# A two-block transformer step on one core: split weights in a ring of 512-row chunks, projections by token halves, attentions begun among the value blocks

## The reference, cut to what matters

```python
def hybrid_layer(x, w_in, w_out, ...):          # layers 0 and 1
    proj = x @ w_in                              # 1024 x 3352
    y = concat(retention(...), nsa(...), rg_lru(...))
    return layer_norm(ALPHA * x + y @ w_out, ln_g, ln_b)

# second block: h starts as the output of layer 1
h = h + dsw_mixer(rmsnorm(h), w_qkv 1024 x 4608, w_o 512 x 1024)   # sliding windows, 8 heads x 3 groups
h = h + relu(rmsnorm(h) @ w1)**2 @ w2            # 1024 x 4096, 4096 x 1024
h = h + moba_mixer(rmsnorm(h), w_qkv 1024 x 3072, w_o 1024 x 1024) # 16 heads
h = h + relu(rmsnorm(h) @ w1)**2 @ w2
```

## Time and profile before

| what | us |
|---|---|
| median of 3 runs (lowest, highest) | 1067.41 (1065.91, 1071.02) |
| the profiled execution, from its first to its last instruction | 1066.1 |
| TensorE busy in it | 1002.8 |
| VectorE busy | 629.1 |
| ScalarE busy | 476.3 |
| mean granted TensorE clock, share of full | 0.949 |

### The profile page before, as it was taken

The page is one execution under the profiler, slowest core; times in us unless marked ns, Lnnn a source line. Parts: engine busy times, 40 slices in busy tenths (PEclk is TensorE's granted clock), DMA queues, the critical chain, the costliest instruction groups (busy, mean ns, idle before and its releaser), DMA issues.

```text
span 1066.1 us, 13756 instructions
## 1 busy us (share of the span) xinstructions
PE 1002.8 (94%) x5626; PEld 859.0 (81%) x5626; DVE 629.1 (59%) x1053; ACT 476.3 (45%) x702; POOL 67.4 (6%) x111
## 2 busy tenths in 40 slices
PE   5999999699999888998998999999999999999998
PEld 3888777588878666886978999888787789998886
DVE  2366864666585677862456665444785566665432
ACT  3443453444355454542545544423654536455231
POOL 4270003000000100000100000000001100000000
PEclk9999958899995989998999999999999999999999
DMA  9664106364310626463515556554555235555540
GB/s 264 215 188 140 40 1 115 105 221 157 119 40 1 198 39 227 161 234 69 61 61 176 189 174 215 174 190 165 168 197 178 50 124 183 176 191 197 185 170 39
DMA packets 77743, 154.56 MB, mean 145 GB/s; under 512 B 4440, under 2 KB 6792, under 8 KB 77681
## 3 DMA queue, kind: packets, MB, share of 16 engines
q1 hardware_dynamic: 72080, 141.76, 40.6%
q0 software_dynamic: 5056, 10.88, 6.3%
q10 hardware_dynamic: 544, 1.05, 0.3%
HBM read 152.57 MB, written 1.11 MB: 144 GB/s over the span
## 4 chain that ended last, share of the span: by engine, by line
PE 82%; DVE 8%; DMA 4%; ACT 3%; issue 2%; SPq 0%; DVEq 0%; ACTq 0%
PE ps L542 16%; PE ps L543 16%; PE ps L544 15%; PE ps L562 6%; PE ps L564 6%; PE ps L563 6%; DMA w_raw<-in_w_in 3%; PE ps L699 2%; PE ps L707 2%; PE ps L726 2%; DVE w_lo L1214 2%; DMA w_raw<-in_a_w_qkv 1%; PE ps L729 1%; PE ps L727 1%; PE ps L690 1%
## 5 line engine op out<-in xcount | busy, mean ns | idle before, releaser
L1214 DVE TENSOR_TENSOR w_lo<-w_raw,w_hi 128x2048 fp32r<-128x2048 f32 x136 | 305.8, 2261 | 200.8 <-ACT w_hi L919 200.5
L919 ACT ACTIVATE w_hi<-w_raw 128x2048 fp32r<-128x2048 f32 x136 | 255.3, 1889 | 146.1 <-PE ps L544 123.2
L542 PE MATMUL ps<-w_hi,act_hi 128*128 128x512 f32 (+1 forms) x544 | 218.6, 402 | 21.4 <-DVE w_lo L1214 10.3
L543 PE MATMUL ps<-w_lo,act_hi 128*128 128x512 f32 (+1 forms) x544 | 214.6, 395 | 0.0
L544 PE MATMUL ps<-w_hi,act_lo 128*128 128x512 f32 (+1 forms) x544 | 214.1, 393 | 0.0
L542 PEld LDWEIGHTS ps<-w_hi,act_hi 128*128 128x128 f32 x544 | 106.3, 195 | 46.4 <-issue 15.8
L544 PEld LDWEIGHTS ps<-w_hi,act_lo 128*128 128x128 f32 x544 | 106.0, 195 | 21.8
L543 PEld LDWEIGHTS ps<-w_lo,act_hi 128*128 128x128 f32 x544 | 106.4, 196 | 20.0
L543 PE MATMUL ps<-w_lo,hid 128*128 128x512 f32 x256 | 102.1, 399 | 0.0
L542 PE MATMUL ps<-w_hi,hid 128*128 128x512 f32 x256 | 101.0, 394 | 0.0
L544 PE MATMUL ps<-w_hi,hid 128*128 128x512 f32 x256 | 100.4, 392 | 0.0
(11 more groups left out here) (244 smaller groups left out, 1413.5 us busy)
## 6 DMA issues: line engine op xcount, KB each, us to landing
w_raw<-in_ffn_w SPq DMA_DIRECT2D x64, 1024.0 KB, 5.4
w_raw<-in_w_in SPq DMA_DIRECT2D x24, 1024.0 KB, 5.9
w_raw<-in_a_w_qkv SPq DMA_DIRECT2D x18, 1024.0 KB, 5.7
w_raw<-in_b_w_qkv SPq DMA_DIRECT2D x12, 1024.0 KB, 5.2
w_raw<-in_w_out SPq DMA_DIRECT2D x8, 1024.0 KB, 5.1
w_raw<-in_b_w_o SPq DMA_DIRECT2D x4, 1024.0 KB, 5.9
area<-bias_vec POOLq DMA_DIRECT2D x8, 384.0 KB, 6.5
w_raw<-in_w_in SPq DMA_DIRECT2D x4, 560.0 KB, 3.7
```

The source lines that it names most:

```text
L542: pe.matmul(bank[:, 0:n], ah, wh, start=first, stop=False)
L543: pe.matmul(bank[:, 0:n], ah, wl, start=False, stop=False)
L919: act.activation(w_hi[:, b % AHEAD, 4 * j:4 * j + 4, 0:n], w_raw[:, c % RAW, :, 0:n], ACT.Copy).then_inc(w_hi_done, 1)
L1214: dve.tensor_tensor(lo, w_raw[:, c % RAW, :, 0:n], hi.bitcast(F), ALU.subtract).then_inc(w_lo_done, 1)
```

## The change

The two-block buffers become a ring of four chunks, whose high part may be written as soon as the chunk four before is used (`w_used` for a block's first chunk, `acc_ready` for its last). Tok and feat blocks now go through both token halves, or all four feature groups, with the first chunk and then with the second (`part`). Four pairs of blocks (`out0`, first two of `in1`, `out1`, first two of `dsw`) run the other way (`pair`): both blocks for the first token half, then both for the second, block one in bank 0 and block two in bank 1. The transposes of the layer norm, of the residual and of the first attention pair are moved; the starts of the mixers' attentions are cut in three and put after parts of the last value blocks. ACT now makes the high part of the normalized activations. After the first half of a block ACT and DVE split first and take after. The splits of the four chunks of `out` all come before or in the attention (hooks 5 and 6). The q and k blocks of `moba` alternate. POOL's constants wait for the second chunk's high part. The bias vectors move from after block 1 to after block 2. The store is cut in three. The counts of matmuls and of split operations do not change.

```diff
-    add_blocks("moba", dram["b_w_qkv_2"][0], 0, D, [(512 * i, 512) for i in range(4)], "tok", "qk")
+    add_blocks("moba", dram["b_w_qkv_2"][0], 0, D, [(512 * i, 512) for i in (0, 2, 1, 3)], "tok", "qk")
...
     RAW = 3
-    AHEAD = 2
-
+    RING = 4
+
+
+
+    PAIRED = [FIRST["out0"], FIRST["in1"], FIRST["out1"], FIRST["dsw"]]
+
+    def paired(b):
+        return b in PAIRED or b - 1 in PAIRED
+
+    def bank(b, half):
+
+        return b - max(f for f in PAIRED if f <= b) if paired(b) else half
+
+    def ready(b, half):
+
+        return 2 * (b - bank(b, half)) + 2 * half + bank(b, half) + 1 if paired(b) else 2 * b + half + 1
+
+    def freed(b, half):
+
+        before = sum(d["last"] for d in BLOCKS[:b])
+        return before - bank(b, half) + half + 1 if paired(b) else before + 1
+
+    def used(c):
+
+        return sum(j < BLOCKS[b]["kts"] // 4 - 1 for b, j in CHUNKS[:c + 1])
...
-        w_hi = sb("w_hi", [128, AHEAD, 8, 512], FR)
-        w_lo = sb("w_lo", [128, AHEAD, 8, 512], FR)
+        w_hi = sb("w_hi", [128, RING, 4, 512], FR)
+        w_lo = sb("w_lo", [128, RING, 4, 512], FR)
...
-        BIAS_BLOCK = 1
+        BIAS_BLOCK = 2
+
         def split_after(b, half):
 
-
-            nxt = b + (AHEAD if half else AHEAD - 1)
-            j = 1 - half
-            return [CHUNK0[nxt] + j] if nxt < NB and j < BLOCKS[nxt]["kts"] // 4 else []
+            c = CHUNK0[b + 1] - 1 if half else CHUNK0[b]
+            return [c + RING] if c + RING < len(CHUNKS) and (half or BLOCKS[b]["kts"] == 8) else []
...
+            rows = out[0].rearrange("(t p) d -> p t d", p=128)
+            for half in range(2):
+                sp.wait_ge(acc_free[half], free_count(NB) - 1)
+            sp.dma_start(rows[:, :, 0:512], x[:, :, 0:512]).then_inc(out_done, 16)
             for half in range(2):
                 sp.wait_ge(acc_free[half], free_count(NB))
-            sp.dma_start(out[0].rearrange("(t p) d -> p t d", p=128), x[:, :, :]).then_inc(out_done, 16)
-            sp.wait_ge(out_done, 16)
+                sp.dma_start(rows[:, half, 512:1024], x[:, half, 512:1024]).then_inc(out_done, 16)
+            sp.wait_ge(out_done, 16 * 3)
...
+            pool.wait_ge(w_hi_done, 2)
...
+            def tokens(b, half, ks):
...
+                o = ps[bank(b, half)][:, 0:n]
+                for k in ks:
+                    c = CHUNK0[b] + k // 4
+                    if k == 0 and d["first"] and freed(b, half) > 1:
+                        pe.wait_ge(acc_free[bank(b, half)], freed(b, half) - 1)
+                    if half == 0 and k % 4 == 0:
+                        pe.wait_ge(w_lo_done, c + 1)
+                    if k % 2 == 0:
...
+                    if k == kts - 1:
+                        mm.then_inc(acc_ready, 1)
+                    elif half == 1 and k % 4 == 3:
+                        mm.then_inc(w_used, 1)
...
+            def part(b, j, halfway=None, before_last=None):
+
+                if BLOCKS[b]["form"] == "feat":
+                    features(b, j, halfway, before_last)
+                    return
+                ks = range(4 * j, 4 * j + 4) if BLOCKS[b]["kts"] == 8 else range(2 * j, 2 * j + 2)
+                tokens(b, 0, ks)
+                if halfway:
+                    halfway()
+                tokens(b, 1, ks)
+
+            def pair(b, midway, at):
+
+                for half in range(2):
+                    for i in range(2):
+                        tokens(b + i, half, range(4))
+                        if (half, i) in at:
+                            midway[at.index((half, i))]()
+                        tokens(b + i, half, range(4, 8))
+
+            def gemms(name, count=None, halfway=None, after={}):
+
+                for i, b in enumerate(blocks(name)[:count]):
+                    if paired(b):
+                        if i == 0:
+                            pair(b, [lambda: normalized_acts((name == "dsw") * 1, 1)], [(0, 1)])
+                        continue
+                    for j in range(2):
+                        part(b, j, halfway=halfway if i == j == 0 else None)
+                        if (i, j) in after:
...
+                if p == 0:
+                    pe.wait_ge(qk_norm, (6, 10)[ph - 2])
...
+            def first_scores(ph):
+                staged(ph, 0)
+                unit(ph, 0, "scores")
+
+            def second_scores(ph):
+                unit(ph, 1, "scores")
+                stage_pair(ph, 1)
...
-                gemm(b + 2, [1], midway=lambda: attention_start(l), at=KD)
+                part(b + 2, 1, before_last=lambda: attention_start(l))
...
-                gemms(f"out{l}", midway=lambda: transpose_acts((Y0, Y1)[l], y, 6, (2,)))
-                normalized_acts(l, 0)
-
-            def start(ph):
-                pe.wait_ge(qk_norm, (6, 10)[ph - 2])
-                attention_start(ph)
-
-            gemms("dsw", between=lambda: start(2))
+                pair(FIRST[f"out{l}"], [lambda: transpose_acts((Y0, Y1)[l], y, 6, (2,)), lambda: normalized_acts(l, 0)],
+                     [(0, 0), (1, 1)])
+
+            gemms("dsw", after={(7, 0): lambda: stage_pair(2, 0), (7, 1): lambda: first_scores(2), (8, 0): lambda: second_scores(2)})
             attention(2, DSW_HEADS)
-            gemms("dswo", midway=lambda: transpose_acts(DSW_Y, y, 4, (1,)), at=2)
-            gemms("up0", midway=lambda: residual_acts("dswo", 1))
-            gemms("down0")
-            gemms("moba", midway=lambda: residual_acts("down0", 1), between=lambda: start(3))
+            gemms("dswo", after={(0, 0): lambda: transpose_acts(DSW_Y, y, 4, (1,)), (1, 0): lambda: residual_acts("dswo", 0)})
+            gemms("up0", halfway=lambda: residual_acts("dswo", 1))
+            gemms("down0", after={(7, 0): lambda: residual_acts("down0", 0)})
+            gemms("moba", halfway=lambda: residual_acts("down0", 1),
+                  after={(4, 1): lambda: stage_pair(3, 0), (5, 0): lambda: first_scores(3), (5, 1): lambda: second_scores(3)})
             attention(3, MOBA_HEADS)
             transpose_acts(MOBA_Y, y, KD, (2,))
-            gemms("mobao", midway=lambda: transpose_acts(MOBA_Y, y, KD, (3,)))
-            gemms("up1", midway=lambda: residual_acts("mobao", 1))
+            gemms("mobao", after={(0, 0): lambda: transpose_acts(MOBA_Y, y, KD, (3,)), (1, 0): lambda: residual_acts("mobao", 0)})
+            gemms("up1", halfway=lambda: residual_acts("mobao", 1))
...
+                if c >= RING:
+                    was, part = CHUNKS[c - RING]
+                    if part < BLOCKS[was]["kts"] // 4 - 1:
+                        act.wait_ge(w_used, used(c - RING))
+                    else:
+                        act.wait_ge(acc_ready, ready(was, 1))
...
+            def after_half(b, half, also=None):
+
+                if half == 0 and b == 0:
+                    take(b, 0)
+                    split_hi(RING - 1)
+                elif half == 0:
+                    if also:
+                        also()
+                    splits(b, 0)
+                    take(b, 0)
+                else:
+                    take(b, 1)
+                    if also:
+                        also()
+                    if b == 0:
+                        splits(b, 0)
+                    splits(b, 1)
                 if BLOCKS[b]["use"] == "relu2":
                     l = int(BLOCKS[b]["name"][-1])
                     hidden_hi(HIDDEN0[l] + 2 * (b - FIRST[BLOCKS[b]["name"]]) + half)
 
+            def after_pair(b, begin=None):
+                take(b, 0)
+                if begin:
+                    begin()
+                take(b + 1, 0)
+                splits(b, 0)
+                take(b, 1)
+                splits(b, 1)
+                splits(b + 1, 0)
...
+            def residual_rest(a, gain, i):
+                acts_hi(a, KD, gain, (2, 3), a != MOBA_U)
+                square_sums(i)
...
+                    ins.then_inc(scaled_done, 1)
+                    act.wait_ge(scaled_done, 4 * l + i + 1)
+                    act.activation(act_hi[:, 4 * (i % 2):4 * (i % 2) + 4, 128 * t:128 * t + 128],
+                                   y[:, i % 2, 0:512].rearrange("p (k n) -> p k n", n=128), ACT.Copy).then_inc(at_hi, 1)
...
+                if start == "stage":
+                    staged(0)
+                if start == "first":
+                    softmax(0)
+                if start == "second":
+                    softmax(1)
...
+                units(l, 16, {5: lambda: splits(b + 2, 1), 6: lambda: [lru_gates(l, i) for i in range(3)], 8: lambda: lru_decay(l),
...
-                splits(last_block[f"in{l}"], 1)
-                gemms(f"out{l}")
-                normalized_scaled(l)
-            gemms("dsw", begin=lambda: square_sums(0), early=lambda: units(2, DSW_HEADS, start=True), split=False)
+                for t in range(TT):
+                    splits(FIRST[f"out{l}"] + t, 0)
+                    splits(FIRST[f"out{l}"] + t, 1)
+                    normalized_scaled(l, t)
```

(59 more changed lines are left out.)

318 lines of the change are left out of this document (141 added, 177 removed).

## The result

The changed kernel takes 1088.81 us (median of 4 runs, 1083.45 to 1090.18), the kernel before beside it 1067.61: a ratio of 1.018, interval 1.015 to 1.021. The forecast was 1048, range 1024 to 1064. It is wrong in sign. The ratios in this document leave out one execution, the longest of the first experiment (1097.61 us), because it lies more than 1.5% above the fastest of its kernel.

A forecast was written before the change was run, and what follows sets the result against it. TensorE's matmuls were taken as the bound, so only idle time and low clock could be won back. The terms summed to 19.1 us off 1066.1, 1047.0, forecast as 1048 for the median; range 1024 to 1064.

The forecast's parts named there:

- A: Start of the kernel: the wait for the second chunk and the half clock behind it go, gain 4.5 us.
- C: out0 to in1: 12.1 us of waits and half clock go, new waits of 3.3 and 1.8 come; net gain 5.3.
- D: out1 to dsw: 15.6 us go, new waits (3.3, 2.3, 1.5, 0.9, 4.9) and 1.7 for clock come; gain 1.0.
- E: Start of the dsw attention: 6.3 us go, a 2.7 us wait and 1.7 for the clock come; gain 1.9.
- F: Residual into the next weights, after dswo, down0 and mobao: waits and one half-clock stretch go, gain 8.6 us.
- G: Start of the moba attention: small waits go, a wait of about 1.5 us for the second pair's copy comes; net 0.
- H: End of the kernel: the smaller last store takes 2.6 to 2.8 us, gain 1.2 us.
- R3: Rival, no change: emptying banks makes TensorE wait 0.4 us in each of 41 blocks, 16 us; 1064 us, chance 0.10.
- R1: Rival, faster: three quarters of the 29.2 us of added waits are hidden; 1026 us, chance 0.23.
- B: Both hybrid attentions: one more VectorE split per layer, 0 to 2.3 us each, taken as 1.7; loss 3.4 us.
- R2: Rival, slower: the dsw attention runs at half clock, adding 28 us; 1076 us, chance 0.07.
- R4: Rival, faster: the hybrid attentions keep full clock, gaining 14.8 us per layer; 1018 us, chance 0.04.

The follow-up runs named there:

- the first experiment: Changed kernel with all of the moba attention's start moved to the half of its last value block: 1084.59 us, ratio 1.014.
- the two runs with the same first units: Changed kernel with all attention edits together, 1041.85 us; and that version with the norm's last step moved from unit 8 to unit 10, 1042.39 us.

## Why the prediction was wrong

**What held.** Outside the attentions the sum was good. Stretch by stretch, between the attentions, the change gained 5.4 us up to hybrid 0 (A: 4.5), 5.7 up to hybrid 1 (C: 5.3), 5.9 up to dsw (D and E: 2.9), 4.8 in the two stretches after dsw and moba (F and G: 8.6) and 2.0 behind the last matmul (H: 1.2; its last store landed in 2.1 us, where 2.6 to 2.8 was foretold). That is 23.8 against 22.5 foretold. That the total came so close is luck in part, as D and E gave 3.0 more and F and G 3.8 less. Single waits fell nearly on their sizes: C's 3.3 was 3.31 and its 1.8 was 1.66; D's first two, 3.3 and 2.3, were 3.31 and 2.25; E's 2.7 was 2.74; G's 1.5 was 1.68. D's last three (1.5, 0.9, 4.9) came to one wait of 2.12; that is where D gained more than was said. F was too large: waits of 0.3, 0.6 and 0.7 us were left of those that I had let go whole. R3 did not come: no list of waits shows ScalarE's emptying block by block. R1's hidden waits did not either.

**The step that failed is G**, "about 1.5: 0": a wait at moba's start was priced at its own length. Its length was right (1.68). But the attention behind it took 24.8 us more, because its units ran at half clock to their end. The kernel before with the last part of the start put behind the block, and so with that wait, shows it (58.44 us in place of 34.63). The changed kernel with start and split both moved shows the way back (34.71).

**The same step in B and E.** B counted one more split as up to 2.3 us a layer of VectorE's time. It was 7.5 and 2.8. In the trace the unit waits of up to 1.24 us before had become 1.93 in layer 0 (behind VectorE's parameter chain and a split), 1.51 in layer 0 (behind VectorE's split in unit 6) and 3.04 in layer 1 (behind ScalarE's split in unit 5). 8.9 and 3.3 us came back when these were moved, and the run does not part one from the other. E priced dsw's start up to the wait of 2.7 us, which stands in the dense block and cost little beside itself, and overlooked the split of the last block, which the change puts ahead of unit 0's copies: 1.42 us of wait, and 9.6 of time in all.

**R2 had the mechanism and the wrong place and weight.** It was given to dsw alone, at 0.07, with a price of 28 us. dsw lost 9.6, since its clock came back after 17 us; moba lost 24.8, where R2 was not thought of. Against R2 stood that dsw held 1.00 before; but that was a state with no long wait near its start, and the change adds one. A row pointed there: 29.54 of 30 us busy at 0.50 in attention units says that such units need not bring the clock back. The question to ask was which attention starts with a wait, and not which has been slow so far.

The prediction set the rule of the Trainium skill (TensorE: Matmul & The Clock Gate, Part 1), that sustained activity releases the throttle, against one stretch. In moba the runs do not agree with it either: TensorE busy 58.44 of 58.44 us by the trace, and the clock at 0.51 (the kernel before with the wait at its start). In dsw it came back within the attention, here after a stretch with as full a busy time:

```profile
500.90:517.70 16.80, 16.80 (x72) 15.41 (x71) 3.79 (x10) 5.78 (x13) 1.49 (x2) 0.50 0.62 104
```

What the two attentions differ in, units of three parts or of one, was not tried.

**R4** did not come: the best that any run came to was 46 to 47 us each, and no run had them at full clock. Why they fall is open, and chance has a part in it, as the two runs with the same first units show. Three to four waits of 0.3 to 0.6 us were left in each, which may add up as two of 0.8 did in moba, or something else may do it; no run without any wait in them was made.

## What to carry to other kernels

In this kernel a wait cost little beside its length only where the work behind it brought the clock back. Before moving anything to the start of a stretch of small matmuls, list every wait within the first few microseconds there, splits and copies queued ahead of the first unit among them. Here one wait of 0.82 us was harmless and waits that added up to 1.68 were not; nothing between was tried. If there is more than that, price the stretch at half clock as well, as a second case. When total busy time of TensorE grows at an equal count of matmuls, look at the granted clock first. Keep long passes of the helping engines (here 1.9 and 2.3 us) for behind such a stretch, beside dense matmuls.

## What was not expected of the hardware

After one wait of 1.68 us, with small matmuls on both sides, the clock was halved for 58 to 65 us in moba, while one of 3.31 us in dense matmuls was followed by no more than 3.4 us at 0.50. Two waits of 0.82 and 0.86 us, 1.4 us of matmuls between them, did as much as the one in the execution that was traced; a wait of 0.82 alone was followed by no fall in five executions of moba. In the changed kernel the clock came back only at 876.2 us, though TensorE was busy for 57.76 of the 57.80 us before, and it came back 1.2 us before the first dense matmul (877.42). At half clock nearly the same records of moba's matmuls took 58.44 us against 33.81 in the kernel before, a factor of 1.73 and not the 2 that the prediction took for its short stretches.
